# Key, query and pooling tiles of a hybrid decoder step as seven block products per pair

## What is computed

```python
proj = jnp.einsum('btd,de->bte', u, w_in)
q, k, v, g, p, ga, gb = jnp.split(proj, IN_SPLITS, axis=-1)
qh = rotary(heads(q, RET_DK), pos)
kh = rotary(heads(k, RET_DK), pos) * (RET_DK ** -0.5)
vh = heads(v, RET_DV)
...
S_new = S * c_dec[:, None, None] + jnp.einsum('bhjd,bhjv->bhdv', kc * k_dec[..., None], vc)
...
ya = jnp.einsum('btc,cd->btd', jax.nn.silu(g) * o, w_ret_branch)
pooled, pool_new = pool_mix(p, pool_prev, pos0)
```

## Time and profile before

| | us |
|---|---|
| three runs, median (lowest, highest) | 1185.95 (1185.29, 1187.32) |
| the profiled execution | 1186.07 |
| its span in the trace | 1184.3 |
| TensorE busy | 1139.4 |
| VectorE busy | 376.3 |
| ScalarE busy | 169.0 |
| GpSimd busy | 57.3 |

### The profile page before, as it was taken

How to read it: one execution, slowest core, us unless ns; L and a number is a source line. 1 busy time by engine, 2 the same in 40 slices (tenths; PEclk the granted TensorE clock), 3 DMA queues, 4 the chain that set the end, 5 groups by cost and what they waited for, 6 DMA issues and landing times.

```text
span 1184.3 us, 14904 instructions
## 1 busy us (share of the span) xinstructions
PE 1139.4 (96%) x5835; PEld 578.0 (49%) x5835; DVE 376.3 (32%) x843; ACT 169.0 (14%) x376; POOL 57.3 (5%) x77
## 2 busy tenths in 40 slices
PE   9999999999999999999989999989999989999997
PEld 7889999984434334343333333333333333333432
DVE  4358874752122222221212121212121212121222
ACT  2121231030111111111101010101111111010112
POOL 3154110000000000000000000000000000000000
PEclk9999999999999999999999999999999999999999
DMA  9772789798999999999999999999999999999996
GB/s 321 229 241 72 249 270 386 251 367 329 419 426 431 425 428 430 432 424 434 422 430 431 429 430 434 421 431 429 437 424 430 424 430 430 434 425 432 425 421 244
DMA packets 66807, 455.18 MB, mean 384 GB/s; under 512 B 4321, under 2 KB 39597, under 8 KB 45760
## 3 DMA queue, kind: packets, MB, share of 16 engines
q1 hardware_dynamic: 64544, 447.99, 91.9%
q0 software_dynamic: 1872, 5.95, 1.5%
q10 hardware_dynamic: 344, 0.61, 0.1%
HBM read 448.65 MB, written 6.11 MB: 384 GB/s over the span
## 4 chain that ended last, share of the span: by engine, by line
PE 66%; DMA 31%; SPq 1%; DVE 1%; issue 0%; ACT 0%; DVEq 0%; ACTq 0%
PE psum L1326 23%; DMA ring<-in_w_down 23%; PE psum L1337 12%; PE psum L1096 10%; DMA ring<-in_w_gate_up 8%; PE psum L1236 7%; PE psum L1413 4%; PE psum L1393 1%; PE psum L1447 1%; PE psum L1123 1%; PE psum L1403 1%; SPq L676 1%; PE psum L1448 1%; PE psum L1422 1%; DMA consts<-in_consts 0%
## 5 line engine op out<-in xcount | busy, mean ns | idle before, releaser
L1326 PE MATMUL psum<-ring,x_T 128*64 128x512 f32 x1004 | 454.1, 598 | 9.2 <-DMA ring<-in_w_gate_up 8.5
L1327 PE MATMUL psum<-ring,x_T 128*64 128x512 f32 x994 | 449.0, 598 | 0.0
L1326 PEld LDWEIGHTS psum<-ring,x_T 128*64 128x64 f32 x1004 | 130.6, 137 | 273.5 <-issue 251.4
L1337 PE MATMUL psum<-ring,act_T 128*64 128x512 f32 x960 | 219.2, 610 | 24.0 <-DMA ring<-in_w_down 24.0
L1337 PEld LDWEIGHTS psum<-ring,act_T 128*64 128x64 f32 x960 | 70.8, 140 | 160.5 <-issue 141.8
L1327 PEld LDWEIGHTS psum<-ring,x_T 128*64 128x64 f32 x994 | 129.2, 137 | 0.0
L2375 DVE TENSOR_TENSOR h_raw<-psum,params 128x512 f32<-128x512 f32 x32 | 22.1, 692 | 299.4 <-PE psum L1393 299.4
L2392 DVE TENSOR_TENSOR z_T<-z_T,psum 128x264 f32<-128x264 f32 x112 | 43.0, 426 | 203.9 <-PE psum L1448 203.9
L1236 PE MATMUL psum<-ring 128*128 128x280 f32 (+1 forms) x384 | 92.0, 395 | 0.6 <-issue 0.6
L1236 PEld LDWEIGHTS psum<-ring 128*128 128x128 f32 x384 | 71.6, 190 | 15.5 <-issue 1.0
L1413 PE MATMUL psum<-normed,one_hot 128*128 128x512 f32 x168 | 74.4, 592 | 0.0
(11 more groups left out here) (322 smaller groups left out, 940.5 us busy)
## 6 DMA issues: line engine op xcount, KB each, us to landing
ring<-in_w_gate_up SPq DMA_DIRECT2D x32, 4096.0 KB, 31.7
ring<-in_w_gate_up SPq DMA_DIRECT2D x59, 2048.0 KB, 28.4
ring<-in_w_down SPq DMA_DIRECT2D x56, 2048.0 KB, 33.4
ring<-in_w_in SPq DMA_DIRECT2D x21, 1024.0 KB, 6.5
ring<-in_w_down SPq DMA_DIRECT2D x12, 1024.0 KB, 27.9
spare<-in_w_gate_up SPq DMA_DIRECT2D x5, 1280.0 KB, 36.7
ring<-in_state_ret POOLq DMA_DIRECT2D x8, 512.0 KB, 7.5
ring<-v_rows SPq DMA_DIRECT2D x8, 512.0 KB, 7.1
```

What stands on the lines that cost most here:

```text
L1326: mm(psum[0:CAP, 2 * j + n], x, gate, start=first, stop=final)
L1327: last = mm(psum[CAP:P, 2 * j + n], x, up, start=first, stop=final)
L1337: last = mm(psum[j * CAP:(j + 1) * CAP, 4 + n], hidden[:, j, 4 * h + i], w, start=h == 0 and i == 0, stop=h == 1 and i == 3)
```

## The change

Tiles 8 to 19 (k, q, p) become six pairs as well, pairs 0 to 5; the gate pairs are now 6 to 17 (GATE_FROM is 6). The early pairs use halves of 140 columns, for q too, which before had 264 columns in all. VectorE makes the weight sums of pairs 0 to 2 among the v tiles, GpSimd those of pairs 3 to 6 (four operations each, into free buffers), VectorE those from pair 7. The sums of u are made once for halves of 140, and again for halves of 132 ahead of the gates (`gate_x_sums`). Chunks of tiles 8 to 19 are free once product 4 of their pair is done. The rotation works in place on the pair's parts (`rope`), ScalarE makes two swapped copies in place of three copies (`take_early`) and takes the turned k (`take_turned`). `keep_part(g, ...)` of pairs 2 to 5 waits for `roped`, as pairs g and g-2 share a buffer. `rank_one` moves from GpSimd to ScalarE: four scaled copies of 128 x 256 per state, at the places in RANK_ONE_AT, counted from the first gate pair.

```diff
+_aux(K0 + 1, ("hist",), (6,))
 for _j in range(4):
-    _aux(_j + 10, ("k", _j), (4 + _j % 2,))
...
+    _aux(K0 + 4 + _j // 2 * 2, ("k", _j), (6 - _j % 2 * 2,))
+_aux(K0 + 9, ("s_meta",), (4, 5, 6, 7))
+_aux(K0 + 10, ("s_next", 0), (6, 7))
+_aux(K0 + 11, ("score", 0), (4,))
+_aux(K0 + 11, ("score", 1), (6,))
...
+SUMS_BEFORE = {4: 0, 5: 2, 6: 1, **{g: g - 2 for g in range(GATE_FROM + 3, GATES)}, GATES + 1: GATES - 1, GATES + 2: GATES, GATES + 3: GATES + 1}
+RANK_ONE_AT = {1: (0,), 2: (1,), 3: (2,), 4: (3, 4), 5: (5,), 6: (6, 7)}
...
 # GpSimd
-            step.wait()
-            for b in range(4):
-                rank_one(b)
...
+            def weight_sums(g):
+
+                G, w, sums = nc.gpsimd, group_chunk(g), w_sums[g]
+                wait_group_chunk(pool, g)
+                pool.wait_ge(w_more_ready, 2 * g)
+                if g in SUMS_BEFORE:
+                    pool.wait_ge(product_done, PRODUCT_AT[SUMS_BEFORE[g], 7])
+                G.tensor_tensor(sums[1], w[:, 0:HK, 0:P], w[:, 0:HK, P:2 * P], ALU.subtract).then_inc(w_two_ready, 1)
+                pool.wait_ge(w_two_ready, 2 * g + 1)
+                G.tensor_tensor(w[:, 0:HK, P:2 * P], w[:, 0:HK, P:2 * P], w[:, HK:KD, P:2 * P],
+                                ALU.add).then_inc(w_two_ready, 1)
...
+            for g in (3, 4):
+                weight_sums(g)
             pool.wait_ge(consts_in, 32)
             pool.wait_ge(aux_took, AUX_AT[("k", 3)] + 1)
             nc.gpsimd.tensor_scalar(k_meta, k_few, const("meta_dec"), None, ALU.mult).then_inc(k_meta_ready, 1)
             step(nc.gpsimd.tensor_copy(k_cols, k_T[:, :, NPR:NT]))
+            for g in (5, GATE_FROM):
+                weight_sums(g)
 # TensorE
+            def early_groups():
+
+                for g in range(GATE_FROM):
+                    product(g, 1)
+                    product(g, 2)
+                    if g > 0:
+                        product(g - 1, 3)
+                    if g < GATE_FROM - 1:
+                        for a in AUX_AFTER[K0 + 2 * g]:
+                            aux(a)
+                    product(g, 6)
+                    product(g, 7)
+                    if g > 0:
+                        product(g - 1, 4)
+                    if g == GATE_FROM - 1:
+                        aux(("s_next", 0))
+                    product(g, 5)
+                    if g < GATE_FROM - 1:
+                        for a in AUX_AFTER[K0 + 2 * g + 1]:
+                            aux(a)
+                g = GATE_FROM - 1
+                aux(("score", 0))
+                product(g, 3)
+                aux(("score", 1))
+                product(g, 4)
...
 # product(g, 7)
+                    if g == GATE_FROM - 1:
+                        pe.wait_ge(aux_took, AUX_AT[("s_meta",)] + 1)
 # ScalarE: keep_part
+                elif 2 <= g < GATE_FROM and i != 5:
+                    act_e.wait_ge(roped, 2 * (g - 2) + (1 if i == 1 else 2))
...
+            def rank_one(b):
+
+                act_e.wait_ge(pool_step, 1)
+                act_e.wait_ge(spread_in[b % 4], 16 * (b // 4 + 1))
+                for h in range(H):
+                    last = A(spread_v[:, b % 4, h], spread_v[:, b % 4, h], ACT.Copy, scale=k_cols[:, h, b:b + 1])
+                last.then_inc(rank_one_ready, 1)
...
 # ScalarE: take_groups, at the end of each gate pair
                     keep_part(g, 5)
-                    if g > 0:
+                    if g > GATE_FROM:
                         take_quarters(g - 1)
+                    for b in RANK_ONE_AT.get(g - GATE_FROM, ()):
+                        rank_one(b)
...
 # VectorE
+            def early_groups():
+
+                for g in range(GATE_FROM):
+                    if g >= 2:
+                        rope(K0 + 2 * g - 3)
+                    if g == 0:
+                        aux(("v", 7))
+                    if g == GATE_FROM - 1:
+                        aux(("s_meta",))
+                    finish_first(g)
+                    if g > 0:
+                        finish_second(g - 1)
+                    if 0 < g < GATE_FROM - 1:
+                        rope(K0 + 2 * g - 2)
+                    finish_third(g)
+                    if g == 0:
+                        aux(("hist",))
+                g = GATE_FROM - 1
+                dve.wait_ge(roped, 8)
+                aux(("s_next", 0))
+                aux(("score", 0))
+                finish_second(g)
```

More of the change, by code:

```diff
@@ L164 @@
     _aux(_j + 1, ("v", _j), (4 + _j % 2,))
+_aux(4, ("b_gu",), (7,))
+_aux(K0 + 1, ("hist",), (6,))
 for _j in range(4):
-    _aux(_j + 10, ("k", _j), (4 + _j % 2,))
[L167 to L172, removed]
+    _aux(K0 + 4 + _j // 2 * 2, ("k", _j), (6 - _j % 2 * 2,))
[3 more added lines that the diff above has]
+_aux(K0 + 11, ("score", 1), (6,))
 _aux(G0, ("o", 0), (4, 5))
@@ L237, in group_of_chunk @@
     kind, c = CHUNKS[i]
-    if kind == "in" and c >= G0:
-        return (c - G0) // 2
+    if kind == "in" and c >= K0:
+        return (c - K0) // 2
     if kind == "ret":
@@ L1090, in product @@
                     pe.wait_ge(w_more_ready, 2 * g + 2)
-                    bank, a, b = total, sums[:, 2], x[:, high, second]
+                    bank, a, b = total, sums[2], x[:, high, second]
                 else:
                     pe.wait_ge(quarter_ready, QUARTER_AT[g, 22])
-                    bank, a, b = extra, w[:, high, P:2 * P], x_sums[:, 2]
+                    if g == GATE_FROM:
+                        pe.wait_ge(x_sums_ready, 8)
+                    bank, a, b = extra, w[:, high, P:2 * P], xs[:, 2]
                 for k in range(HK):
-                    last = mm(psum[:, bank, 0:HALF], a[:, k], b[:, k], start=k == 0 and i in (1, 2, 7),
+                    last = mm(psum[:, bank, 0:h], a[:, k], b[:, k], start=k == 0 and i in (1, 2, 7),
                               stop=k == HK - 1, skip_group_check=i not in (1, 2, 7))
@@ new lines, in rank_one, with take_early_groups @@
+            def rank_one(b):
[4 more added lines that the diff above has]
+                last.then_inc(rank_one_ready, 1)
+            def take_early_groups():
+                for g in range(GATE_FROM):
+                    keep_part(g, 1)
+                    if g > 0:
+                        take_early_sum(g - 1)
+                    keep_part(g, 6)
+                    if g > 0:
+                        take_early(g - 1, 0)
+                    if g in (2, 3):
+                        for j in range(2 * g - 4, 2 * g - 2):
+                            take_turned(j)
+                    if g > 0:
+                        take_early(g - 1, 1)
+                    keep_part(g, 5)
+                g = GATE_FROM - 1
+                take_early_sum(g)
+                take_early(g, 0)
+                take_early(g, 1)
@@ L2023, in gate_groups @@
+            def gate_groups():
+                gate_x_sums()
+                aux(("score", 1))
+                for g in range(GATE_FROM, GATES):
                     finish_first(g)
@@ L2102, in branch_groups @@
                 for part in (1, 2, 3):
[L2103 removed]
+                    sum_of_halves(gate_a, out_diff, 3, part)
             few = NS + NM
```

337 lines of the change are left out of this document (195 added, 142 removed).

## The result

The changed kernel takes **1202.47 us** (median of four runs, 1201.62 to 1204.89), the kernel before 1185.62 on the same chip: a ratio of **1.0143, 95% interval 1.0125 to 1.0161**. It is slower, as forecast, but by 16.9 us and not by 4.6: outside the range of 1184.5 to 1193. The profiled execution of the changed kernel took 1202.02 us (span 1200.5), that of before 1186.07 (span 1184.3).

The account below looks back on a forecast made before the run. The mixer was taken as bound by TensorE's unbroken chain of matmuls, the experts by their weight stream starting behind it. From 1186.07 us, -4.37 + 0.4 + 3.3 + 0.5 + 4.7 = +4.5 gave 1190.6, range 1184.5 to 1193.

Parts of the forecast that it names:

- TensorE's saving with the second score's wait: Key, query and pooling tiles as pairs save TensorE 4.37 us; the second score waits 0.4 us behind the last early pair.
- GpSimd's sums against the rotations: In pairs 1 to 5, GpSimd's weight sums hold up VectorE's rotations, so TensorE waits 3.3 us (0 to 5).
- two rank-one products behind pair 4: At the gates, ScalarE's two products there make product 6 of gate pair 5 wait 0.5 us (0 to 0.8).
- row 7 behind ScalarE: ScalarE waits for row 7's load, so product 6 of gate pair 7 comes 4.7 us late (3.9 to 5.5).
- Product 7 of pair 5: Last early pair: this product waits 1.9 us for the copy of s_meta, late behind VectorE's held-up query rotations.
- every meeting at its worst: Upper bound of 5 us on TensorE's waits where GpSimd's sums meet VectorE's rotations.
- Hidden at nothing: VectorE's sums, ScalarE's copies, later loads and GpSimd's stores are covered by other work; losing a cover would cost tenths.
- One rank-one product fits: At the gates, ScalarE has 2.9 us of room per pair, enough for one such product without TensorE waiting.
- Rival 1: Rotations are not held up by GpSimd's sums: the sum without 3.3 us, 1187.3 us; chance 0.15.
- Rival 2: At the gates, row 7 lands in time or its wait falls on nobody: without 4.7 us, 1185.9; chance 0.12.
- Rival 4: Product records of 140 columns cost TensorE more, say 125 ns each: 1192.6 us; chance 0.62 together with the forecast.
- Rival 3: No rotation hold-up and no row 7 wait, so TensorE's saving is gained: 1182.6 us; chance 0.11.

Follow-up runs that it names:

- e7: The changed kernel with each of GpSimd's sixteen weight sums of pairs 3 to 6 replaced by two fills with zeros, which read nothing; 1191.52 us.
- e2: The changed kernel with ten filler matmuls, results unused, ahead of product 6 of the eighth gate pair, where TensorE stood idle; 1201.3 us.
- e1: The changed kernel with rank-one products 4 to 7 back on GpSimd, 0 to 3 staying on ScalarE; 1192.93 us.
- e4: The changed kernel with ScalarE's rank-one products, except product 3, moved behind keep_part of product 1 of a later gate pair; 1192.74 us.
- e5: The changed kernel with the edits of e3 and e4 together; 1185.9 us, ratio 0.9996 against the kernel before.
- e6: The kernel before with only the eight rank-one products moved to ScalarE, at the change's places; 1194.11 us.
- e3: The changed kernel with GpSimd's weight sums kept apart from the rotations: pair 3's ahead of the state loads, those of pairs 4 to 6 waiting for rotations; 1197.38 us.
- e8: The changed kernel with the edits of e5 and three exchanges in VectorE's order; 1182.78 us, ratio 0.9975 against the kernel before.

## Why the prediction was wrong

Its direction and each mechanism that it put into its sum held, and four of its five terms came out at their size. Its sum was 4.5 us; the marks give 15.6 at E. Term by term:

| step | forecast | measured | from |
|---|---|---|---|
| TensorE's saving with the second score's wait | -4.37 + 0.4 | -3.9 | K to G of e7 less before |
| GpSimd's sums against the rotations | 3.3 (0 to 5) | 7.6 | K to G of changed less e7, without the clock |
| two rank-one products behind pair 4 | 0.5 (0 to 0.8) | 0.5 | the hole of 0.33 and its refilling |
| row 7 behind ScalarE | 4.7 (3.9 to 5.5) | 4.8 | the hole of 4.62 and its refilling |
| third gate pair | 0 | 1.6 | the hole of 1.44 and its refilling |
| low clock behind the key holes | 0 | 1.8 | K to G of changed less e2 |
| low clock behind the row 7 hole | 0 | 3.0 | 164.32 to 171.57 against 4.3 before; e2 |

They add up to 15.4; 0.2 at E and the 0.6 in the experts I don't assign. (One figure of the prediction doesn't come out of its own terms: with rotations at 1.2 and landing at 3.9 its sum is 1187.7, not 1188.4. The range given starts lower, so nothing hangs on it.)

**The rotations, mis-sized: 7.6 for 3.3.** The step that failed is the one that priced a meeting at one GpSimd operation. It put pair 3's sums on the rotation of key head 0 and called head 1 "some 1.2 us late: wait 0.6". But the sums ran through the whole rotation, and *each* of its three operations was held: 1.23, 1.51 and 1.40 us, 4.1 in all against 1.3 alone. The prediction had 3.6 us for a covered rotation just above its list of meetings, and did not use it there. The second omission is that the two key heads of a pair are waited for one after the other: TensorE came to head 0's transposes at 58.4 us, just where the prediction had it (58.5), waited for head 0, transposed, and then waited again for head 1, whose rotation had only then begun. So the four heads cost 0.76, 0.89, 1.06 and 0.90 of idle time, 4.2 us with refilling, for 1.2 forecast. Third, the holes ahead of products 6 and 5 of pair 4 (1.8 us) were not in the sum: `keep_part` waits for `roped` there too, and the prediction followed that wait in pair 5 alone. Product 7 of pair 5 was about right (1.3 for 1.9). How the waits of pairs 4 and 5 divide differs between executions: in e1, e2 and e4, which run the same program up to G, pair 4 has no hole of over 0.2 us and the one ahead of product 7 is 2.9 us. The upper bound of 5 fell with the same choice: it counted "every meeting at its worst", but took in only the meetings that the prediction lists.

That GpSimd's side is hardly lengthened in turn, as the prediction read from the earlier trace rows, held: with no rotation beside it a sum took 1.27 or 1.28 us in e5, and in the changed kernel 1.27 to 1.36 beside the first rotation and 1.53 at most. The prediction had interpolated 1.1.

**The third gate pair: 1.6 for nothing.** "Hidden at nothing" holds the step that failed: the new sums of u were asked only whether they come in time for the first gate pair, which they do. But they push VectorE's queue back. They stand in it behind G (2.6 us), and behind them the taking of the second score (1.2 us), which stood ahead of G before; the taking of s_next (1.4 us) has gone the other way. `finish_second` of the first gate pair stands 19.41 us behind G where it stood 18.50 before, 0.91 later. ScalarE waits for it, then makes row 0's rank-one product, and only then keeps the part that TensorE needs (timelines of VectorE, before and after, and of ScalarE):

```profile
112.52 0.29 DVE L2007 TENSOR_TENSOR z_T<-psum,z_T 128x132 f32<-128x132 f32 x1
...
118.97 0.28 DVE L2137 TENSOR_TENSOR z_T<-psum,z_T 128x132 f32<-128x132 f32 x1
...
119.35 0.42 ACT L1768 ACTIVATE z_T<-z_T 128x264 f32<-128x264 f32 x1 [1.40 <-DVE z_T L2137]
119.68 1.69 ACT L1814 ACTIVATE ring<-ring 128x256 f32<-128x256 f32 x4
121.27 0.25 ACT L1751 COPY z_T<-psum 128x132 f32<-128x132 f32 x1
```

The two causes add: the copies alone make 0.53 us (e6), VectorE's 0.91 on top 1.44, which is the hole measured. In e3 VectorE is 1.93 later than before, and 0.53 + 1.93 is the 2.46 measured there; in e7 it is 1.40 later, and the sum of 1.93 is a little over the hole of 1.70. Without the copies in front there is no hole here (e4), and once G comes 7 us earlier VectorE, held up by GpSimd as in e3, makes 0.88 by itself (e5). With `finish_second` moved forward that hole is gone too (e8). "One rank-one product fits" rested on a slack of 2.9 us read in the seventh pair; the third pair, where VectorE is still busy with the scaling of `o`, has less.

**The clock: 4.8 for nothing.** No part of the prediction asked what a hole does to the matmuls behind it. TensorE had no hole in the mixer of the kernel before, but its experts did show the effect: the earlier trace rows has a clock of 0.97 where TensorE idles for 13.5 us of 200, and in that stretch a hole of 2.51 us that ends at 654.16 is followed by 0.50 from 656 to 658 us (behind one of 2.53 us that ends at 612.04 it stayed at 1.00). The hole for row 7 was forecast right, and its tail of 3.0 us was left out. The page "TensorE: Matmul & The Clock Gate" of the Trainium skill says in Part 1, "The HAM clock gate", that the lower clock is the default and that activity releases it. The trace agrees: filler matmuls in the hole kept the clock at 1.00 in e2, where the changed kernel has 0.50.

**Rivals.** Rival 1 (no hold-up) is refuted by the 1.23 to 1.51 us. Rival 2 (row 7 in time) by the 4.19 us wait. Rival 4 (dearer records) by K to G of e7, 46.97 for 46.88. Rival 3, pure gain at 1182.6, is what the change is worth once nothing stands in its way: e8 measured 1182.78, with the slack that the rival asked for made by re-ordering.

Open: what decides whether holes of 1 to 3 us bring the clock down. Up to G, e1, e2 and e4 run the changed kernel's program. The key holes were followed by 0.50 in the changed kernel and by 1.00 in the other three. Behind a hole of 2.93 and 2.91 us ahead of product 7 of pair 5 the clock fell to 0.50 in e1 and e4, and behind one of the same 2.93 us it stayed at 1.00 in e2. With one such fall, wherever it stands, K to G is 56.31 to 56.36 us, and without any 54.52. In the third gate pair it fell behind 2.46 us (e3) and not behind 1.44 to 1.70 (the changed kernel, e1, e2, e7). Behind the hole of 4.5 to 4.7 us it fell in all four kernels that have it. So the 1.8 us of the table is what the clock cost in the profiled execution of the changed kernel, and another execution may have been spared it.

## What to carry to other kernels

Moved work is priced in three places: the queue it joins (who stands behind it there, above all if it waits for a load), the engine whose operands it competes for (every operation in the cover, not one per meeting), and whoever is late next. Then add to each hole on TensorE of some microseconds the slow matmuls behind it, and look for their price wherever the trace at hand has such a hole. And before a good idea is dropped: here a handful of re-orderings within the queues of GpSimd, ScalarE and VectorE, none of which takes any arithmetic away, turned 1.4% slower into 0.25% faster.

## What was not expected of the hardware

- Idle time of 4.6 us on TensorE costs 3.0 us more in the full stretch behind it (granted clock 0.50 from 164 to 170 us), and 2.4 to 2.6 in e3, e6 and e7. Even holes of about 1 us, two pairs of them 10 us apart, were followed by 0.50 at 72 to 74 us in the changed kernel, though nearly the same holes in e2 were not.
- GpSimd writing without a break beside VectorE's two-input operations lengthens them by nothing (0.44 and 0.45 us), while a GpSimd operation that reads holds up the VectorE operation that meets it until about its own end; even one of 8 columns, 0.17 us alone, took 1.12 us beside a sum in the changed kernel.
